# An encoder block with product-key experts: bare queries, gates on ScalarE, row transposes behind the splits, squares in sixteen buffers, final scaling on VectorE

## What is computed

```
def hybrid_layer(h, ...):
    u = rmsnorm(h, norm1_w)
    proj = u @ w_in + b_in                      # q, k, v, o, gates, glu, branch gates
    y_a = mlstm_branch(q, k, v, o, ...)         # 8 heads
    y_b = conv_branch(glu, conv_w, ...)         # 31 taps
    h = h + (sigmoid(g_a) * y_a + sigmoid(g_b) * y_b) @ w_o
    return h + peer(rmsnorm(h, norm2_w), ...)

def peer(tb):                                    # per token
    qry = (tb @ w_q).reshape(..., 8 heads, 2, 128)
    s = einsum('thpd,pkd->thpk', qry, sub_keys)  # 128 keys per half
    sv, si = top_k(s, 16)
    cand = sv[:, :, 0, :, None] + sv[:, :, 1, None, :]
    top, pos = top_k(cand, 16)
    gates = softmax(top)
    z = einsum('thed,td->the', expert_u[eidx], tb)
    return einsum('the,thed->td', gates * gelu(z), expert_v[eidx])

h = hybrid_layer(concat([meta_tokens, x]), ...)
return rmsnorm(h, final_norm_w)[:, 16:]
```

## Time and profile before

| what | us |
|---|---|
| median of 3 runs | 4336.75 |
| lowest, highest | 4336.17, 4338.55 |
| profiled execution | 4336.15 |
| its span, first to last instruction | 4333.4 |
| TensorE busy | 4250.4 (98%) |
| VectorE busy | 3412.7 (79%) |
| ScalarE busy | 1285.8 (30%) |
| POOL busy | 917.3 (21%) |
| mean granted clock of TensorE | 0.993 |

### The profile page before, as it was taken

One profiled execution on the slowest core, in us unless ns is written; L12 is line 12 of the kernel. 1 busy time (PEld: TensorE's weight loads), 2 busy tenths in 40 slices (PEclk: granted clock), 3 DMA queues, 4 the chain that ended last, 5 costly groups with the idle time before them and its releaser, 6 DMA issues.

```text
span 4333.4 us, 65477 instructions
## 1 busy us (share of the span) xinstructions
PE 4250.4 (98%) x24970; PEld 3891.5 (90%) x24970; DVE 3412.7 (79%) x4189; ACT 1285.8 (30%) x1230; POOL 917.3 (21%) x804
## 2 busy tenths in 40 slices
PE   8999999999999999999999999999999999999998
PEld 5878887989989888887889999999999999999998
DVE  5776766788888844555898999978886989999996
ACT  4222222221212233223223444432323323333333
POOL 0111111000100120011111333344441222222223
PEclk9999999999999999999999999999999999999999
DMA  6888887789899986989844888999997989999995
GB/s 222 306 288 305 286 309 250 249 288 291 283 291 286 319 302 220 312 285 340 282 153 148 327 324 336 356 379 380 375 369 281 353 333 370 363 381 380 371 355 192
DMA packets 395168, 1326.18 MB, mean 306 GB/s; under 512 B 29472, under 2 KB 202528, under 8 KB 279360
## 3 DMA queue, kind: packets, MB, share of 16 engines
q1 hardware_dynamic: 298352, 892.67, 59.6%
q0 software_dynamic: 62224, 391.99, 22.9%
q10 hardware_dynamic: 34496, 40.37, 2.6%
HBM read 1130.49 MB, written 328.53 MB: 337 GB/s over the span
## 4 chain that ended last, share of the span: by engine, by line
PE 85%; DVE 8%; issue 3%; DMA 2%; POOL 1%; ACT 0%; SPq 0%; DVEq 0%; ACTq 0%; POOLq 0%
PE bank L850 27%; PE bank L851 27%; PE bank L852 27%; DVE w_lo L1592 2%; DVE u_row L2130 1%; DVE hot_j L2140 1%; DMA u_row<-u_rows,z_index 1%; PE bank L955 1%; PE bank L962 1%; PE bank L1091 1%; PE bank L931 1%; DVE hot_i L2136 1%; POOL cand L748 0%; PE bank L953 0%; DMA u_row<-u_rows,z_index_x 0%
## 5 line engine op out<-in xcount | busy, mean ns | idle before, releaser
L1176 ACT ACTIVATE w_hi<-w_raw 128x2048 fp32r<-128x2048 f32 x432 | 826.5, 1913 | 1969.1 <-PE bank L852 1799.2
L1592 DVE TENSOR_TENSOR w_lo<-w_raw,w_hi 128x2048 fp32r<-128x2048 f32 x432 | 993.9, 2301 | 260.0 <-ACT w_hi L1176 257.7
L850 PE MATMUL bank<-x_split,w_hi 128*128 128x352 f32 (+1 forms) x3072 | 1063.2, 346 | 17.2 <-DVE w_lo L1592 7.6
L851 PE MATMUL bank<-x_split,w_hi 128*128 128x352 f32 (+1 forms) x3072 | 1060.9, 345 | 0.0
L852 PE MATMUL bank<-x_split,w_lo 128*128 128x352 f32 (+1 forms) x3072 | 1056.1, 344 | 0.0
L850 PE MATMUL bank<-x_hi,w_hi 128*128 128x264 f32 (+1 forms) x2688 | 868.9, 323 | 0.0
L852 PE MATMUL bank<-x_hi,w_lo 128*128 128x264 f32 (+1 forms) x2688 | 863.5, 321 | 0.0
L851 PE MATMUL bank<-x_lo,w_hi 128*128 128x264 f32 (+1 forms) x2688 | 862.5, 321 | 0.0
L851 PE MATMUL bank<-x_split_o,w_hi 128*128 128x352 f32 x2048 | 656.8, 321 | 0.0
L850 PE MATMUL bank<-x_split_o,w_hi 128*128 128x352 f32 x2048 | 655.2, 320 | 0.8 <-DVE z_group L2019 0.8
L852 PE MATMUL bank<-x_split_o,w_lo 128*128 128x352 f32 x2048 | 654.3, 319 | 0.0
(11 more groups left out here) (315 smaller groups left out, 4089.2 us busy)
## 6 DMA issues: line engine op xcount, KB each, us to landing
v_rows<-v_blocks SPq DMA_DIRECT2D x128, 1024.0 KB, 10.3
w_raw<-u_blocks SPq DMA_DIRECT2D x128, 1024.0 KB, 8.0
w_raw<-v_blocks SPq DMA_DIRECT2D x128, 1024.0 KB, 7.3
w_raw<-w_proj SPq DMA_DIRECT2D x112, 1024.0 KB, 7.2
u_raw_a<-u_blocks SPq DMA_DIRECT2D x99, 1024.0 KB, 8.3
u_rows<-u_turned_a SPq DMA_DIRECT2D x396, 256.0 KB, 5.6
g_scratch<-g_chunk SPq DMA_DIRECT2D x11, 2048.0 KB, 13.3
z_scratch<-z_stage POOLq DMA_DIRECT2D x112, 176.0 KB, 5.7
```

The lines of the kernel that those rows point to most:

```text
L850: pe.matmul(dst, whi, xhi, start=start, stop=False)
L851: pe.matmul(dst, whi, xlo, start=False, stop=False)
L1176: act.activation(WH[s][:, :], RAW[s][:, :], ACT.Copy).then_inc(w_hi, 1)
L1592: dve.tensor_tensor(WL[s][:, :], RAW[s][:, :], WH[s][:, :].bitcast(F32), ALU.subtract).then_inc(w_lo, 1)
```

## The change

1. The squares of x get a buffer each (`SQ1`, over the memory of x_lo); VectorE adds them by twos and for three of four groups by fours, TensorE makes 10 calls in place of 16. The warm-up of the Sqrt table stands ahead of the squares.
2. A `u_turn` ahead of the splits of B1 goes behind `lo(B1 + 1)`. Likewise at Q1, where it goes behind `lo(C1 + 17)` and stands right ahead of the next `u_turn`.
3. Queries are copied bare from PSUM by ScalarE. rstd is turned so that it is a value per token (four transposes of TensorE, a copy of 128x4), and scales inside the Exp, which becomes four ACTIVATEs. `SV0` and `SV1` get two buffers. VectorE's order within a pair of blocks becomes keys, lo, candidates of the head before, keys, lo.
4. Zone 17 comes ahead of the table transposes on TensorE; on VectorE `z_scale(16)` comes ahead of `rt_done`.
5. hot_j of four tokens is one TENSOR_TENSOR without the gate; ScalarE multiplies the gates in, with four ACTIVATEs for a group (`gated`), right behind the copy of the same group of the frame before; TensorE waits for these (`hot_sc`). `hots(n + 1)` stands behind `z_scale(n)`, ahead of the second dot.
6. X_FLUSH is 26 instead of 25, V_FIRST 27 instead of 26.
7. VectorE alone does the final scaling of all 16 tiles, in their order.

```diff
@@ start: ScalarE, VectorE
-                if kt >= 4:
-                    act.wait_ge(ss_use, kt // 2 * 2 - 2)
-                act.activation((sq0, sq1, sq2, sq3)[kt % 4][:, :], R1[:, kt, :], ACT.Square).then_inc(sq_rdy, 1)
+                act.activation(SQ1[:, kt, :], R1[:, kt, :], ACT.Square).then_inc(sq_rdy, 1)
+            for q in range(4):
+                for k in range(2):
+                    t = 4 * q + 2 * k
+                    dve.wait_ge(sq_rdy, t + 2)
+                    dve.tensor_tensor(SQ1[:, t, :], SQ1[:, t, :], SQ1[:, t + 1, :], ALU.add).then_inc(sq_pair, 1)
+                if q < 3:
+                    dve.wait_ge(sq_pair, 3 * q + 2)
+                    dve.tensor_tensor(SQ1[:, 4 * q, :], SQ1[:, 4 * q, :], SQ1[:, 4 * q + 2, :], ALU.add).then_inc(sq_pair, 1)
@@ start of B1, VectorE (the last turn moves from the block before)
             split(r2tile, 16)
             lo(B1 + 1, 1)
+            u_turn(U_B2 // 2, 0, u_a2)
             some(last_taps, 11)
             b1(0, 0, 0)
@@ start of Q1, VectorE
             residual(14, 7, 0)
             lo(C1 + 16, 0)
-            u_turn((U_C1 + 12) // 2, (U_C1 + 12) % 2, u_c1)
             split(r1tile, 64, range(KT - 1), N2W)
             residual(15, 7, 1)
             split(r1tile, 64, [KT - 1], N2W)
             lo(C1 + 17, 1)
-            u_turn((U_C1 + 13) // 2, (U_C1 + 13) % 2, u_c1)
+            for u in range(2):
+                u_turn((U_C1 + 12 + u) // 2, (U_C1 + 12 + u) % 2, u_c1)
@@ queries: VectorE before, ScalarE after
-                dve.tensor_tensor(qry[u][:, :], bk[u][:, :], rsB[:, :], ALU.mult).then_inc(evac_v, 1)
-                lo(n + (Q1 + 2), u)
+                act.activation(qry[u][:, :], bk[u][:, :], ACT.Copy).then_inc(qry_rdy, 1)
+                hi2(Q1, n - u, u)
@@ queries: TensorE; VectorE
+            pe.wait_ge(rsB_rdy, 1)
+            for t in range(TT):
+                m = pe.transpose(A[0][:, P * t:P * t + P], rsB[:, P * t:P * t + P], ident[:])
+            m.then_inc(rsT_rdy, 1)
+            query(2, 0)
+            def top_keys(h, odd, cands):
+
+                keys(2 * h, 0, odd)
+                lo(2 * h + (Q1 + 4), 0)
+                if cands:
+                    candidates(h - 1)
+                keys(2 * h + 1, 1, odd)
+                lo(2 * h + (Q1 + 5), 1)
@@ softmax, ScalarE
-            act.activation(GA[:, :, :], GA[:, :, :], ACT.Exp).then_inc(sm_exp, 1)
+            for t in range(TT):
+                act.activation(GA[:, t, :], GA[:, t, :], ACT.Exp, scale=rsT[:, t:t + 1]).then_inc(sm_exp, 1)
@@ tables: TensorE; VectorE
             zone(Z_TABLES, 0)
+            zone(Z_TABLES + 1, 1)
 
             pe.wait_ge(rt_done, 1)
...
-            zone(Z_TABLES + 1, 1)
+            z_scale(Z_TABLES, 0, 8 * Z_TABLES)
             dve.wait_ge(v_step, here())
             dve.sem_inc(rt_done, 1)
...
-            z_scale(Z_TABLES, 0, 8 * Z_TABLES)
@@ one-hots: TensorE; ScalarE; VectorE
-                        pe.wait_ge(hot_rdy, 4 * i + 2 * u + g + 1)
+                        pe.wait_ge(hot_sc, 4 * i + 2 * u + g + 1)
+            def gated(m, g):
+                act.wait_ge(hot_rdy, 2 * m + (g + 1))
+                for q in range(4):
+                    o = act.activation(hot_j[g][:, q, :], hot_j[g][:, q, :], ACT.Identity,
+                                       scale=AT[:, ds(TOK * m + (4 * g + q), 1)])
+                o.then_inc(hot_sc, 1)
+
-                    for q in range(4):
-                        tok = TOK * n + 4 * g + q
-                        o = dve.tensor_scalar(hot_j[g][:, q, :], iota[:, :], JT[:, tok:tok + 1], AT[:, tok:tok + 1],
-                                              ALU.is_equal, ALU.mult)
-                    o.then_inc(hot_rdy, 1)
+                    dve.tensor_tensor(hot_j[g][:, :, :], iota[:, :].unsqueeze(1).to_broadcast((P, 4, P)),
+                                      JT[:, TOK * n + 4 * g:TOK * n + 4 * g + 4].unsqueeze(2).to_broadcast((P, 4, P)), ALU.is_equal
+                                      ).then_inc(hot_rdy, 1)
@@ end, VectorE
-            for k in range(OUT_V):
+            for k in range(KT):
                 dve.scalar_tensor_tensor(OUT[:, k, :], OUT[:, k, :], col[:, FNW, k:k + 1], rsB[:, 0:N3], ALU.mult, ALU.mult
                                          ).then_inc(out_rdy, 1)
```

174 lines of the change are left out of this document (90 added, 84 removed).

## The result

The changed kernel takes 4304.84 us (median of 4 runs, 4301.87 to 4310.45) against 4336.46 for the kernel before, a ratio of 0.9929 with a 95% interval of 0.9913 to 0.9945: 0.7% faster, or 31.6 us between the medians. 4290 was forecast, with a range of 4274 to 4312. The way and the range held, and two thirds of the 46 us came.

A forecast was written before the change was run, and what follows sets the result against it. TensorE, busy 4250.4 of 4333.4 us, was taken as the bound, losing time to waits, mostly for VectorE, and to the lower clock. The terms summed to 46.3 us off 4336.15, giving 4289.9, stated as 4290; range 4274 to 4312.

The forecast's parts named there:

- one-hot term: One-hot frames: merged hot_j and gates on ScalarE give VectorE slack, winning 22.5 us of 28 lost (12 to 27.5).
- start of B1: Moving the transpose behind the splits and a low part removes a 3.6 us stall and 3.0 of clock: 6.3 (4 to 7.5).
- signs for "right": Gate waits under 5 us, frames 9.4 to 9.5, no query wait, B1 and flush under 1, new Q1 wait 5 to 7.
- signs for "wrong": Gates over 0.35 us apart, clock of 0.50 behind one-hot gaps, or VectorE's u_row waits above 8 us.
- Start of Q1: Split stall nearly goes, but two transposes together delay the reciprocal; TensorE waits 4.7 to 6.8 us: -1.5 (-6 to +3).
- Queries: Queries copied by ScalarE end TensorE's 10.0 us of waits, less 0.9 for transposes and 0.3 for Exp: 8.8 (6 to 10).
- Tables: Table transposes: block 17 fills the 6.9 us wait, but z_scale(16) delays the signal: +1 (-1 to +3).
- Flush, start and end: Later flush saves 5.9 us (3 to 5.9), squares at the start 1.0 (0.5 to 1.2), final scaling 2.3 (1.5 to 2.5).
- (a): Rival: one-hot stretch gives half back, 1 to 2.5 us at each of 11 stores of g; 4301 to 4317, chance 0.10.
- (b): Rival: Q1's pair of transposes meets an 11.5 us store (-6) and tables gain nothing (-1); 4296.5, chance 0.12.
- (c): Rival: ScalarE's gate, copy, gate chain bounds one-hot frames, at 0.50 us a gate not 0.29; 4346, chance 0.02.
- (d): Rival: merged hot_j in the one-hot frames runs in a slower mode, 2.1 us a tile; 4381, chance 0.01.

The follow-up runs named there:

- e6: The kernel before with the one-hot part of the change alone (merged hot_j, gates on ScalarE, one-hots ahead of the second dot); 4315.79 us.
- e4: The changed kernel with POOL's store of z of block 16 ahead of its wait for the indices; 4299.22 us.
- e1: The changed kernel with SyncE's two row copies issued ahead of its wait for the moved turn at the start of B1; 4300.24 us.
- e2: The changed kernel with the turn ahead of the splits of B1 again, its old place; 4303.79 us.
- e3: The changed kernel with the second turn at the start of Q1 behind the reciprocal and one low part on VectorE; 4298.65 us.
- e10: e9 with the four row copies of blocks Q1+2 and Q1+3 at the end of SyncE's Q1 stage; 4286.35 us.
- e8: The kernel before with only the flush of v_sums and the second part's start one block later; 4330.24 us.
- e7: The changed kernel with each gate made in two ACTIVATEs of 64 columns, eight for a group in place of four; 4332.8 us.
- e5: The changed kernel with the edits of e1, e3 and e4, and SyncE's row copies ahead of its wait for the turn at Q1 too; 4295.29 us.
- e9: The changed kernel with the edits of e1, e3 and e4 alone; 4289.58 us.
- e12: The changed kernel again, unedited, run beside later versions on one chip; 4304.61 us.

## Why the prediction was right, and where its sizes were off

**The range.** The time is in the range, but the range held by its width. The one-hot term came to 10.4 and 13.2 us (12 to 27.5 stated) and that of the start of B1 to 0.2 and 2.8 (4 to 7.5 stated). The bounds don't follow from their own words either: with every upper value but the two uncertain ones the sum is 54.1 us, 4282 and not 4274, and with the three lower values that are named it is 28.5, 4307.6 and not 4312. The measured 4304.84 lies inside these too. Of the prediction's own signs for "right" two failed: TensorE waited 9.5 us for gates and not under 5, and 2.8 us at the start of B1 and not under 1. Two of its signs for "wrong" appeared: a clock of 0.50 behind a gap in the one-hot stretch, and, narrowly, waits of VectorE for u_row of 8.5 us against 8.0.

**One-hot frames** (22.5 forecast, 10.4 and 13.2 found). The mechanism and the price were right: hot_j as one TENSOR_TENSOR has a median of 686 ns and a start-to-start time of 0.60 (0.61 forecast), gates of 387 ns in groups of 1.2 us, undisturbed frames of 9.36, and alone (e6) it gave 22.0. What the term lacked is what another part of the change did to it: z_scale(16) ahead of the signal moves nothing on POOL, but the block behind it now starts earlier and meets a store that POOL holds behind the gathers. I had written for the tables that z_scale(16) waits for a store, and didn't ask the same of z_scale(18). The one-hots had been moved behind z_scale, so that this wait held them too. e4 shows it. This is 7.7 us; the rest is the wait for rows beside two stores of g, 10.4 and 7.4 us in the two profiles where 5 had been left.

**Start of B1** (6.3 forecast, 0.2 and 2.8 found). The step that failed is "VectorE pays for the transpose afterwards, ahead of b1(0), where it has just enough time". VectorE had the time. The turn's stores are in SyncE's queue with 2 MB of copies and the next w_raw behind them. SyncE stood idle for 12.6 us ahead of them with the DMA engines half used (0.58), and the load left 4.0 us late and landed late behind the copies (e1). And the 3.0 us of clock were not a fixed cost of the stall (e2): with the old order the clock fell in three profiles and not in the fourth.

**Start of Q1** (+1.5 forecast, +2.9 and +2.8 found). The steps came as written, and the one that was mis-sized is the wait for the first turn's stores: 10.5 us, where 7.4 to 9.5 were taken and 11.5 had been seen before. The first turn came at 2030.51 (2032.4 forecast), and behind it a stall of 5.4 + 1.3 us (4.7 to 6.8) with 6.8 us at half clock. The whole lies inside the range of the term. e3 shows that the reciprocal behind the second turn cost half of it, and e10 that most of the rest was traffic: copies that nothing there needs.

**Queries** (8.8 forecast, 7.4 found). No wait for a query is left. The pair took 24.03 in place of the 24.5 forecast. The lead did run out, at the change to zones, where TensorE stood 0.6 and 3.4 us with half clock behind it. The prediction had counted five pairs of query blocks and not the step from 11.9 to 7.6 us a block behind them. No run has this part alone, so that its 7.4 us are read from the stage.

**Tables** (1.0 forecast, 3.7 found). The 6.9 us went. Of the 6.8 us at half clock 3.4 stayed, now behind the wait of 1.8 us. The signal came earlier than I said: z_scale(16) started at 2373.76, not at 2380, because the wait for the store was 3.8 us and everything lay 6 us earlier. TensorE waited only 1.8 and 1.1 us for low parts. It may be that these 2.7 us more were lost again in the first frames, where z_scale(18) waits for a store that leaves at its own time; no run separates them.

**Flush, start and end** (5.9, 1.0, 2.3 forecast; 5.9, 1.0 to 1.6, 2.2 to 2.4 found). As written. e8 has the flush alone; in five other runs 1.5 of the 5.9 were lost to the clock again. The start and the end were not run alone.

**The rivals.** (a) is the nearest: the one-hot stretch gave back half and the time is in its 4301 to 4317, but its mechanism, late gathers at each of the eleven stores of g, holds for two stores only (2 to 5 us beyond the 5 that were left for it); the rest was the store of z. (b) did not occur as a pair: the store was nearly as slow (10.5 us), but the tables gained. (c) did not occur, and e7 shows that a little more work on ScalarE brings it on. (d) is refuted: 686 ns. The Trainium skill, "VectorE: DVE Perf Modes", section "The perf-mode tier table (the rule you actually need)", gives the rates for 2048 elements; here four operations of 128 columns cost 1.11 us in the kernel before and one of 512 costs 0.69, so that the 2.1 us scaled from those rates was three times too high. On the gates, the row's 0.29 us was right (1.23 to 1.28 for the first start to the last end of four), and the estimate of 0.41 that the Trainium skill gives ("ScalarE: Activation LUTs", section "Rules for kernel authors") was not what a chain costs; it is near the 0.387 us that one gate lasts.

## What to carry to other kernels

When an operation moves, follow the queue of each engine that waits for it, the DMA-issuing ones first: a SyncE that stands at a store holds every load behind it, and the price appears two blocks later under another name ("waits for w_lo"). Then ask of each part of a change what the others did to its neighbours; here a part worth 22 us alone gave 10 to 16, in the main because a store that had been early enough was so no longer. Copies that nobody needs soon are best issued where the DMA engines have room: the same edit won 3.6 to 6.2 us at one stage start, where their share had been 0.58, and lost 5.3 at another (e5 against e9), where it was 1.04.

## What was not expected of the hardware

The clock fell to 0.50 behind a stall of 3.63 us at the start of B1 in the kernel before, and did not behind one of 3.17 us at the same place in e2 (1.00 over the 7 us behind it). A stall of 2.8 us at block 115 in the changed kernel was followed by 3.4 us at 0.50, and at the same block one of 1.84 us in e3 was, and one of 1.71 in e12 was not. At each of the two places the longer stalls were the ones that cost clock (3.63, 4.20 and 4.96 us against 3.17; 1.84 to 2.78 against 1.71), but what was enough at one place was not at the other. And 3.2 to 4.0 us after the start of the flush's 32 products of 32 columns, without a wait, the clock fell to 0.50 for 3.4 us in five profiles (e1, e3, e4, e5, e10), and not in the seven others with the later flush. So a gap's length alone does not tell whether clock goes with it, and a term for the clock should be given as a chance.

An ACTIVATE of 64 columns (334 ns, 0.24 us from one to the next) takes nearly the time of one of 128 (387 ns, 0.29). And issuing the four stores of a turn took SyncE 2.51 us in the earlier trace rows, 6.13 us in e3, and 10.28 us in e5 at the same place, with 2 MB of copies issued in the 12 us ahead.
